# A two-layer hybrid decoder step: the mixers' small products in array parts, the state decay on ScalarE, the means ahead of the pooling products

## The reference, cut to what matters

```python
z = hn @ w_in                       # u | q | k | v | g, 512 columns each
# retention, 8 heads of 64, chunks C = 128, state S
sc    = einsum('bnhd,bmhd->bhnm', qc, kc) * dmask        # scores
inner = einsum('bhnm,bmhe->bnhe', sc, vc)
cross = einsum('bnhd,bhde->bnhe', qc, S) * xi            # outputs = inner + cross
S     = S * g_c + einsum('bmhd,bmhe->bhde', kc * zeta, vc)   # chunk states
# sample rows: one step from a given state: S * gamma + k v
mu  = mean(o); var = mean((o - mu)**2)                   # per head
o   = (o - mu) * rsqrt(var + eps) * silu(g)
# pooling: windowed mean of u minus u, times w_pool per group of 128, times scale
h   = h + concat(pool_out, o) @ w_o
```

## Time and profile before

| | |
|---|---|
| time, median of 3 runs | 918.82 us (913.53, 918.82, 919.22) |
| span of the profiled execution, first to last instruction | 916.9 us |
| its mean granted TensorE clock | 0.986 of full speed |
| TensorE busy | 891.9 us (97%) |
| VectorE, ScalarE, GpSimd busy | 707.6, 523.2, 188.4 us |

### The profile page before, as it was taken

How to read it: one execution, slowest core, us unless ns; L and a number is a source line. 1 busy time by engine, 2 the same in 40 slices (tenths; PEclk the granted TensorE clock), 3 DMA queues, 4 the chain that set the end, 5 groups by cost and what they waited for, 6 DMA issues and landing times.

```text
span 916.9 us, 14294 instructions
## 1 busy us (share of the span) xinstructions
PE 891.9 (97%) x5873; PEld 775.1 (85%) x5873; DVE 707.6 (77%) x791; ACT 523.2 (57%) x585; POOL 188.4 (21%) x196
## 2 busy tenths in 40 slices
PE   6999999999999999999999999999999999999995
PEld 6999899999999999999877777777777777776795
DVE  5798486555565588786569989889898989888976
ACT  5331464443445356322438778787877778786762
POOL 5449141100110012675211410002000100010011
PEclk9999899999999999998999999999999999999998
DMA  9984266536554554953227999999999999999801
GB/s 340 356 290 122 71 232 212 187 134 225 179 185 166 181 188 142 297 177 118 107 90 249 403 345 351 401 392 394 364 393 362 397 386 370 401 356 384 317 1 49
DMA packets 50291, 236.46 MB, mean 258 GB/s; under 512 B 4802, under 2 KB 8034, under 8 KB 42496
## 3 DMA queue, kind: packets, MB, share of 16 engines
q1 hardware_dynamic: 44544, 215.46, 63.0%
q0 software_dynamic: 4960, 18.96, 7.1%
q10 hardware_dynamic: 720, 1.10, 0.3%
HBM read 226.34 MB, written 8.55 MB: 256 GB/s over the span
## 4 chain that ended last, share of the span: by engine, by line
PE 78%; DVE 11%; DMA 4%; issue 4%; ACT 3%; POOL 0%; ACTq 0%; SPq 0%; DVEq 0%; POOLq 0%
PE bank L710 14%; PE bank L711 13%; PE bank L712 13%; DVE wlo L1520 6%; PE bank L1055 6%; PE bank L1056 6%; PE bank L1057 6%; PE bank L1081 4%; PE bank L1080 4%; PE bank L1082 4%; ACT whi L1252 1%; DMA xt<-summed 1%; DMA xg<-tokens,from_row 1%; DMA summed<-ys,to_row 1%; PE bank L840 1%
## 5 line engine op out<-in xcount | busy, mean ns | idle before, releaser
L1520 DVE TENSOR_TENSOR wlo<-raw,whi 128x1408 fp32r<-128x1408 f32 (+2 forms) x292 | 467.3, 1631 | 97.5 <-ACT whi L1252 97.3
L1252 ACT ACTIVATE whi<-raw 128x1408 fp32r<-128x1408 f32 (+2 forms) x292 | 395.4, 1378 | 158.3 <-PE bank L712 88.4
L710 PE MATMUL bank<-xh,whi 128*128 128x264 f32 x672 | 195.3, 291 | 9.0 <-DVE xl L1531 8.3
L711 PE MATMUL bank<-xl,whi 128*128 128x264 f32 x672 | 193.0, 287 | 0.0
L712 PE MATMUL bank<-xh,wlo 128*128 128x264 f32 x672 | 192.8, 287 | 0.0
L1055 PE MATMUL bank<-whi,xeh 128*96 128x512 f32 (+1 forms) x384 | 143.8, 374 | 1.1 <-DVE wlo L1520 0.6
L1056 PE MATMUL bank<-wlo,xeh 128*96 128x512 f32 (+1 forms) x384 | 143.6, 374 | 0.0
L1057 PE MATMUL bank<-whi,xel 128*96 128x512 f32 (+1 forms) x384 | 143.2, 373 | 0.0
L710 PEld LDWEIGHTS bank<-xh,whi 128*128 128x128 f32 x672 | 129.2, 192 | 10.3 <-DVE wlo L1908 8.2
L711 PEld LDWEIGHTS bank<-xl,whi 128*128 128x128 f32 x672 | 129.3, 192 | 0.1
L712 PEld LDWEIGHTS bank<-xh,wlo 128*128 128x128 f32 x672 | 128.6, 191 | 0.0
(11 more groups left out here) (260 smaller groups left out, 1285.6 us busy)
## 6 DMA issues: line engine op xcount, KB each, us to landing
raw<-in_moe_w_gate SPq DMA_DIRECT2D x32, 1408.0 KB, 8.8
raw<-in_moe_w_up SPq DMA_DIRECT2D x32, 1408.0 KB, 9.7
raw<-in_moe_w_down SPq DMA_DIRECT2D x40, 1024.0 KB, 8.5
raw<-in_w_in SPq DMA_DIRECT2D x17, 1024.0 KB, 5.6
raw<-in_ffn_w_down SPq DMA_DIRECT2D x16, 704.0 KB, 4.2
raw<-in_ffn_w_gate SPq DMA_DIRECT2D x10, 1024.0 KB, 4.9
raw<-in_ffn_w_up SPq DMA_DIRECT2D x10, 1024.0 KB, 4.9
raw<-in_w_o SPq DMA_DIRECT2D x8, 1024.0 KB, 10.7
```

The lines of the kernel that those rows point to most:

```text
L710: pe.matmul(out, w_hi, x_hi, start=start, stop=False)
L711: pe.matmul(out, w_hi, x_lo, start=False, stop=False)
L1252: act.activation(unit_hi(u), unit_raw(u), ACT.Copy).then_inc(hi_ready, 1)
L1520: dve.tensor_tensor(unit_lo(u), unit_raw(u), unit_hi(u).bitcast(F32), ALU.subtract).then_inc(lo_ready, 1)
```

## The change

The scores of both heads of a block are one step for TensorE, alternating between the lower and the upper 64 rows of the array, and land in two banks. `vpad` becomes `vrow`, without zeros: outputs and chunk states are done per head with 64 weight columns, so that the heads' results stand in the lower or upper 64 rows of a bank (column parts). `S1` and `S2` become one step `S`. The variances use 32 weight columns per head pair (four column parts), and the spreading uses two rows of each quarter (four row parts). The decay of the sample state moves from GpSimd to ScalarE. The means come ahead of the pooling products, `va` ahead of `w_o`, and a square root on one element ahead of the pooling products' copies. `FULL` counts the marks on `side_full`, since some steps now give two or four. Waits, constants and sizes that follow are left out:

```diff
-         ["vs", "vt0", "vt1", "sc00"],
-         ["sc01", "kt0", "kt1", "win", "o0", "sc10", "sc11"],
-         ["S1", "S2", "tail", "o1"],
-         ["qS", "wp0", "wp1", "wp2", "wp3"] + [f"mu{c}" for c in range(RC)],
+         ["vs", "vt0", "vt1"],
+         ["sc00", "sc01", "kt0", "kt1", "win", "o0", "sc10", "sc11"],
+         ["S", "tail", "o1"],
+         ["qS"] + [f"mu{c}" for c in range(RC)] + ["wp0", "wp1", "wp2", "wp3"],
          ["va"] + [f"rb{c}" for c in range(RC)]]
...
                 elif name[:2] == "sc":
+                    pe.wait_ge(side_free, i + 1 - 3)
                     for c in range(RC):
-                        mm = pe.matmul(b[:, c * CH:(c + 1) * CH], qk[rows, 1, c, blk:blk + CH],
-                                       qk[rows, 0, c, blk:blk + CH], start=True, stop=True)
+                        for hp in range(2):
+                            rows = slice(hp * HD, (hp + 1) * HD)
+                            mm = pe.matmul(bank[side_bank(l, f"{name[:3]}{hp}")][:, c * CH:(c + 1) * CH],
+                                           qk[rows, 1, c, blk:blk + CH], qk[rows, 0, c, blk:blk + CH], start=True, stop=True)
...
+                elif name == "S":
+                    for blk in range(2):
+                        for c in range(RC):
+                            for a in range(2):
+                                mm = pe.matmul(b[a * HD:(a + 1) * HD, at:at + HD], kz[:, blk, d:d + HD], vrow[:, blk, c, a, :],
+                                               start=True, stop=True)
                 elif name in ("o0", "o1"):
                     if blk:
-                        pe.wait_ge(side_free, SIDE[l, "S1"] + 1)
+                        pe.wait_ge(sbd_ready, l + 1)
                     for c in range(RC):
-                        pe.matmul(out, vc[:, 0:P], sc[:, 0, c, :], start=True, stop=False)
-                        mm = pe.matmul(out, vc[:, HD:HD + P], sc[:, 1, c, :], start=False, stop=not blk)
+                        for a in range(2):
+                            mm = pe.matmul(b[a * HD:(a + 1) * HD, c * CH:(c + 1) * CH], vrow[:, blk, c, a, :], sc[:, a, c, :],
+                                           start=True, stop=not blk)
                         if blk:
-                            mm = pe.matmul(out, sbd[:, c, :], qxi[:, c, :], start=False, stop=True)
+                            for a in range(2):
+                                own = slice(a * HD, (a + 1) * HD)
+                                mm = pe.matmul(b[own, c * CH:(c + 1) * CH], sbd[:, c, own], qxi[:, c, :], start=False, stop=True)
...
+                    pe.wait_ge(osq_ready, RC * (l + 1))
                     for c in range(RC):
-                        mm = pe.matmul(b[0:HEADS, 0:T], hvar[:, c, :], osq[:, c, :], start=(c == 0), stop=(c == RC - 1))
+                        mm = pe.matmul(b[c * LANE:(c + 1) * LANE, 0:T], C("hvar"), osq[:, c, :], start=True, stop=True)
                 elif name[:2] == "rb":
-                    mm = pe.matmul(b[:, 0:T], hrow[:, int(name[2]), :], rvar[:, :], start=True, stop=True)
+                    lane = slice(int(name[2]) * LANE, int(name[2]) * LANE + 2)
+                    mm = pe.matmul(b[:, 0:T], hrow[lane, :], rvar[lane, :], start=True, stop=True)
...
-                pe.wait_ge(side_free, SIDE[l, "wp3"] + 1)
+                side_step(l, "va")
                 for first_row in (0, PC):
-                    if first_row:
-                        for c in range(RC):
-                            side_step(l, f"rb{c}")
                     for m in range(4):
                         for k in range(first_row, first_row + PC):
+                            if k < PC and m == 0:
+                                pe.wait_ge(side_free, SIDE[l, f"wp{k}"] + 1)
...
                         elif m == 1:
-                            side_step(l, "va")
+                            for c in range(RC):
+                                side_step(l, f"rb{c}")
...
+                    if j == 7:
+                        act.wait_ge(layer_in, 64 * (l + 1))
+                        for c in range(RC):
+                            act.activation(S[:, :, c, :], S[:, :, c, :], ACT.Copy,
+                                           scale=C("gamma")[:, c:c + 1]).then_inc(s_decayed, 1)
...
+                act.activation(rvar[0:1, 0:1], C("eps", 1), ACT.Sqrt)
...
-                pool.tensor_tensor(S[:, :, :, :], S[:, :, :, :],
-                                   C("gamma").unsqueeze(1).unsqueeze(3).to_broadcast([P, NS, RC, HD]),
-                                   ALU.mult).then_inc(s_decayed, 1)
```

More of the change, by code:

```diff
@@ L55 @@
 PAD = 16
+LANE = 32
 UNIT = 2048
@@ L89, in constants @@
     put("hmean", np.where(p[:, None] // HD == p[None, :] // HD, f(1.0 / HD), f(0)))
-    heads = 2 * np.arange(RC)[None, :, None] + p[:, None, None] // HD
-    put("hvar", np.where(heads == np.arange(HEADS)[None, None, :], f(1.0 / HD), f(0)))
+    put("hvar", np.where(p[:, None] // HD == np.arange(LANE)[None, :], f(1.0 / HD), f(0)))
     put("upper", np.where(p[:, None] < p[None, :], f(1), f(0)))
@@ L317 @@
 TOKEN_ORDER = (0, 2, 4, 1, 3, 5)
-SIDE = {}
-_at = 0
+LANES = {"o0": 2, "o1": 2, "S": 2, "va": RC}
+SIDE, FULL = {}, {}
+_at = _full = 0
 for _l in range(DEPTH):
@@ L324 @@
             _at += 1
+            _full += LANES.get(_s, 1)
+            FULL[_l, _s] = _full
+    for _s, _last in [("sc00", "sc01"), ("sc10", "sc11")] + [(f"rb{_c}", f"rb{RC - 1}") for _c in range(RC)]:
+        FULL[_l, _s] = FULL[_l, _last]
 SIDE[DEPTH, "norm1"] = _at
+FULL[DEPTH, "norm1"] = _full + 1
 SIDE_MOE = _at
@@ L391, in program @@
         rstd = place("rstd", [P, T])
-        hrow = place("hrow", [HEADS, RC, P])
+        hrow = place("hrow", [P, P])
         wr = place("wr", [P, DC, NE])
@@ L421, in program @@
         kz = place("kz", [P, 2, 512], F32, mix_at)
[L422 to L424 removed]
+        vrow = place("vrow", [P, 2, RC, 2, HD], F32, mix_at + 4096)
+        sc = place("sc", [P, 2, RC, CH], F32, mix_at + 4096 + 4096)
+        qxi = place("qxi", [P, RC, CH], F32, mix_at + 4096 + 4096 + 4096)
         oc = place("oc", [P, RC, T], F32, x_at)
@@ L428, in program @@
         og = place("og", [P, RC, T], F32, x_at + 8 * RC * T)
-        rvar = place("rvar", [HEADS, T], F32, x_at + 12 * RC * T)
+        rvar = place("rvar", [P, T], F32, x_at + 12 * RC * T)
         fh = place("fh", [P, EC, T], F32R, arena)
@@ L1182, in _ @@
                     for name in AFTER[j]:
-                        if name != "norm1":
+                        if name not in ("norm1", "sc01", "sc11"):
                             side_step(l, name)
-                pe.wait_ge(side_free, SIDE[l, "wp3"] + 1)
+                side_step(l, "va")
                 for first_row in (0, PC):
-                    if first_row:
-                        for c in range(RC):
-                            side_step(l, f"rb{c}")
                     for m in range(4):
@@ L1432, in _ @@
                             act.activation(sg[:, c, :], sg[:, c, :], ACT.Silu).then_inc(silu_g, 1)
-                for g in range(PC):
-                    i = SIDE[l, f"wp{g}"]
-                    act.wait_ge(side_full, i + 1)
-                    act.activation(mh[:, g, :], bank[4 + i % 4][:, 0:T], ACT.Copy,
-                                   scale=pscale[:, l, g:g + 1]).then_inc(mix_hi, 1)
                 for c in range(RC):
@@ L1441, in _ @@
                     act.activation(osq[:, c, :], oc[:, c, :], ACT.Square).then_inc(osq_ready, 1)
-                i = SIDE[l, "va"]
-                act.wait_ge(side_full, i + 1)
-                act.activation(rvar[:, :], bank[4 + i % 4][0:HEADS, 0:T], ACT.Sqrt, bias=C("eps", HEADS)).then_inc(stdv_ready, 1)
+                act.activation(rvar[0:1, 0:1], C("eps", 1), ACT.Sqrt)
+                for g in range(PC):
+                    act.wait_ge(side_full, FULL[l, f"wp{g}"])
+                    act.activation(mh[:, g, :], bank[side_bank(l, f"wp{g}")][:, 0:T], ACT.Copy,
+                                   scale=pscale[:, l, g:g + 1]).then_inc(mix_hi, 1)
+                act.wait_ge(side_full, FULL[l, "va"])
+                act.activation(rvar[:, :], bank[side_bank(l, "va")][:, 0:T], ACT.Sqrt, bias=C("eps")).then_inc(stdv_ready, 1)
                 for c in range(RC):
```

79 lines of the change are left out of this document (38 added, 41 removed).

## The result

The changed kernel takes 906.53 us (904.47 to 909.39) against 917.79 beside it: ratio 0.9874, 95% interval 0.9843 to 0.9905. A second set of runs gave 907.71 against 916.33, ratio 0.9893 (0.9863 to 0.9924). So it is faster by 9 to 11 us; the forecast was 911, by 7.3. The first profiled execution took 907.34, with a span of 905.2.

The account below looks back on a forecast made before the run. TensorE, busy 97% of the span, was taken to bound the kernel. Gains of 3.05 us a layer, twice, plus 1.2 once for the hole gave 7.3, so 911 us; 80% range 904.5 to 919.

Parts of the forecast that it names:

- wait at `win`: Before the outputs: `win` needs the first score's bank, which VectorE takes out later; cost 0.4 us a layer.
- states: Chunk states in column parts, 32 records of 64 weight columns: 2.0 instead of 1.78 us, a loss of 0.2 a layer.
- wait for `sbd`: Before `o1`: VectorE's two copies can begin only when all states are done, covered only by the tail; cost 0.6 us.
- hole ahead of `qS`: TensorE's 1.19 us wait for GpSimd's state before L840, layer 0 only; would close with the decay on ScalarE.
- wait behind `qS`: Means, now right behind L840's second half, must wait for VectorE's copies of that result; cost 0.5 us a layer.
- 96 passes of `w_o`: Behind `rb`, the low clock and short waits for `ml` in the second half should go; gain 2.1 us a layer.
- Outputs, scores, `va`, `rb`: Products in array parts, gains a layer: scores 1.42, `o0` 0.76, `o1` 0.55, `va` 0.95, `rb` 1.2 us.
- The first rival: Column parts run in turn, without overlap: 6.6 us lost in all, leaving 918; chance 0.17.
- va in front of w_o: `va` waits for `wp0`'s copies behind squares and table load, partly covered by pooling products; cost 2.2 us in both layers.
- The second rival: The 2.2 us wait lowers the clock, slowing the 24 passes behind `va` by 1.7 us a layer: 914.5; chance 0.13.
- More than summed (906): States overlap too (1.6 us) and the low clock behind L840 fails to come twice (3.4): 906; chance 0.20.
- The slower rival: Every change of column part pauses the engine (0.16 us), 14 us in two layers, column gains gone: 932; chance 0.08.

Follow-up runs that it names:

- e3_pool_first: The changed kernel with pooling products ahead of the means again and ScalarE's copies ahead of the squares, `va` still ahead of `w_o`; 904.48 us, ratio 0.9862.
- e7_xt_later: The changed kernel with GpSimd's third product `xt` at the first experts two weight units later; 907.13 us, ratio 0.9869.
- e11_parts_only: The changed kernel with its array parts and ScalarE decay, but the order of before: pooling first, `va` behind 24 passes, `rb` behind 48; 906.00 us, ratio 0.9872.
- e12_best_xt_seven_later: The changed kernel with pooling ahead of means, `va` behind 12 passes, `rb` behind 36, and GpSimd's third `xt` seven weight units later; 905.46 us, ratio 0.9852.
- e9_before_again: The kernel before, unedited, run again for a second profile; its two mixers took 120.1 us.

## Why the prediction held, step by step

Gains of the two profiles first compared, in us:

| step | forecast a layer | layer 0 | layer 1 |
|---|---|---|---|
| scores | +1.42 | +1.63 | +1.62 |
| wait at `win` | -0.4 | -0.38 | -0.60 |
| `o0` | +0.76 | +0.94 | +0.94 |
| states | -0.2 | +0.70 | +0.71 |
| wait for `sbd` | -0.6 | -0.82 | -0.83 |
| `o1` | +0.55 | +0.76 | +0.76 |
| hole ahead of `qS` | +1.19 once | +1.24 | 0 |
| clock behind the first half of `qS` | 0 | +1.48 | +1.55 |
| wait behind `qS` | -0.5 | -2.04 | -0.63 |
| pooling and means with the wait for `va` | -2.2 | -2.07 | -1.95 |
| `va` | +0.95 | +1.29 | +1.30 |
| `rb` | +1.2 | +1.58 | +1.58 |
| 96 passes of `w_o` | +2.1 | +2.42 | +2.55 |

The direction and every sign but one came out, and the time lies in the range. The size came out too small: 7.3 us were forecast, and the two sets measured 11.3 and 8.6. The overlap was priced too low, as nothing for the states and too little for the rest, 4.4 us in all. The half clock behind `qS` was put at no change, and it varies from one execution to the next; how near a single pair comes to the sum is partly luck. Of the signs that the prediction named, the hole in layer 0 is gone, and the clock behind `rb` was full in both layers of both profiles. The wait ahead of `va` was 0.47 and 1.68 (0.85 and 0.86 in the second profile) instead of 2.2. And the low clock did appear in a new place, the experts, which was to mean that the prediction is wrong; but it is there in the third profile of before as well, so the change does not bring it. In detail:

- **States, the one wrong sign.** I priced 32 records with 64 weight columns by L840's 2.05 and left the overlap to a rival. They took 1.08. Having taken overlap for the outputs, I should have taken it here too: 1.8 us over both layers.
- **Outputs, scores, `va`, `rb`** overlap somewhat better than the 1.2 (or 1.0) I charged: 16 records in 1.02 to 1.09, 8 in 0.6. Over both layers that is 2.6 us more than forecast.
- **The first rival is dead.** Column parts run at once where they alternate (1.02 against 1.51 for `o0`), and even in turn `o0` did not take the 2.1 that I had priced. The Trainium skill's "TensorE: Matmul & The Clock Gate", Part 3, lets weight loads overlap running matmuls only where the row groups differ. Read as I read it, that would have left the column parts in turn; the measurement decides. The gain of 2.38 times that the Trainium skill gives there for three column parts agrees better.
- **va in front of w_o.** The mechanism is as forecast, and moving the load bears it out. Its price shows in another form where the pooling products themselves ran at half clock, which filled part of the wait.
- **The second rival did not come as stated.** The 24 passes behind `va` took 3.1 us in both layers, as before, though TensorE had waited 0.47 and 1.68 ahead of it. Behind `qS` a wait may lengthen the stretch at half clock: in layer 0, with 1.97 us of waiting, it is twice as long as in layer 1, with 0.56. But the stretch comes without any wait too (e3_pool_first), so a wait is not needed for it.
- **Wait behind `qS`, -2.04 in layer 0.** I counted VectorE's two copies, and not what stands ahead of them on VectorE: products beside GpSimd's state adds (one took 2.36, alone it takes 0.17), then a `wlo` and the two products for `sg`:

```profile
80.91 2.36 DVE L1694 TENSOR_TENSOR wsum<-wsum,const 128x16 f32<-128x16 f32 x1
...
84.76 2.28 DVE L1547 TENSOR_TENSOR wlo<-raw,whi 128x2048 fp32r<-128x2048 f32 x1
...
87.64 0.17 DVE L1637 COPY o<-bank 64x32 f32<-64x32 f32 x1
```

  They stood there before, too, with three such long products, but TensorE came later then. Its second half of `qS` began here:

```profile
90.69 2.03 PE L840 MATMUL bank<-qm,S 128*64 128x2 f32 x32
```

  The copies came 5.1 earlier than before (87.64 against 92.75), this half of `qS` 6.5 earlier (84.15 against 90.69). With 1.48 less at half clock just before, TensorE came earlier than VectorE; where that stretch was slow again (layer 0 of e7_xt_later) the wait was 0.56. These two rows of the table belong together.
- **More than summed (906)** hit the time, but only one of its two reasons holds: the states overlap. The clock behind the first half of `qS` varies: it was low in five of six places in the three profiles of before and in one of four in the two of the changed kernel. That is too few to tell whether the change makes it rarer or the pair was lucky.
- **The slower rival** (a pause for each change of part) is dead: with fewer changes the kernel is 5.5 us slower than e7_xt_later beside it.

By experiments the gain needs two things: undoing the alternation costs 5.5 us (e5_in_turn) and undoing the decay on ScalarE 5.7 us (e6_decay_on_gpsimd), both against e7_xt_later of the same set, which is not the changed kernel itself. The profiles agree: the mixers took 115.2 and 115.8 there, 109.5 and 110.4 in the changed kernel. The two are not shares that add up. The decay is worth far more than the hole that was seen, because without it the time that the parts save ahead of `qS` is waited off there. The new order of means, `va` and `rb` brings nothing by itself that these runs can tell (e11_parts_only), and pooling first with a later `va` beats it.

What stays open: what decides whether a stretch behind `qS` falls to half clock. No run here tells it.

## What to carry to other kernels

Small products that fill half the array took about two thirds of the time (0.66 to 0.73 for scores, `o0` and states) when neighbours in the queue used different halves, rows or columns; exchanging two loops was enough. Before taking a wait's length for what it is worth to remove it, ask how much earlier its engine will come after the other edits. And take a second profile of both kernels before explaining a difference of 3 us between two: here one pair differed by a collision, and by stretches at half clock, that come and go from one execution to the next.

## What had not been expected of the hardware

- GpSimd and VectorE exclude each other for whole instructions when both work on two tensors in SBUF: `wlo` alone 1.60, beside `xt` up to 3.83 (e12_best_xt_seven_later); `xt` 2.40 to 7.61. In all twelve profiles with a long `wlo` it ended 1.48 or 1.49 behind `xt`, little less than its own length. The Trainium skill's "SBUF — State Buffer", section SBUF: two separate sides, says that whichever of the two starts first keeps the shared ports for its whole instruction and the other is blocked, and the 1.48 and 1.49 agree. What decides when GpSimd gets in stays open: ahead of the long `wlo` VectorE had paused 0.58 in e9_before_again, 0.21 in e5_in_turn, and not at all in e3_pool_first and e12_best_xt_seven_later.
- Half-sized products can beat whole ones: the states in 32 alternating records of 64 weight columns took 1.08, in 16 records of the whole array 1.78, for the same useful result.
